# Expert rows gathered in turned form, features stationary

## The chip, the cores and the metric

The kernel runs on one core of a Trainium2 chip. TensorE (PE) multiplies: each product is a load of weights, the stationary operand, into the array (LDWEIGHTS, shown as the engine PEld), and a pass of the moving operand through it (MATMUL). VectorE (DVE), ScalarE (ACT) and GpSimd (POOL) do the rest, SyncE (SP) issues the DMAs. Products accumulate in the eight banks of PSUM, of 512 floats per partition each; everything else lies in SBUF, 128 partitions wide. The metric is the device time of one launch in microseconds.

## The reference

One layer of a hybrid decoder: a token mixer (RG-LRU and linear attention), then a mixture of experts with 32 experts, of which each token takes 4, and a final norm. 280 tokens (16 meta, 256 of the prompt, 8 samples) with 1024 features go through it. The change lies in the expert part:

```python
def _moe(u, w_router, b_router, w_gu, b_gu, w_down, b_down):
    logits = u @ w_router + b_router
    top_val, top_idx = lax.top_k(logits, TOP_K)      # 4 of 32
    gates = jax.nn.softmax(top_val, axis=-1)
    ...
    def expert_block(args):
        tok, e = args
        xb = u_pad[tok]                               # the rows of expert e
        gu = xb @ w_gu[e] + b_gu[e]                   # 1024 -> 2048
        gate = jnp.minimum(gu[:, :D_FF], SWIGLU_LIMIT)
        lin = jnp.clip(gu[:, D_FF:], -SWIGLU_LIMIT, SWIGLU_LIMIT)
        act = (lin + 1.0) * gate * jax.nn.sigmoid(SWIGLU_ALPHA * gate)
        return act @ w_down[e] + b_down[e]            # 1024 -> 1024
    ...
    y = jnp.zeros((n_tok + 1, d)).at[row_tok].add(y_rows * row_w[:, None])
```

## The kernel before

The mixer, the residual and the router come first, until about 165 us. They leave the normalised tokens in `u2` (three chunks of 128, 128 and 24 rows by 1024 features), and for every token and expert its place among the expert's tokens in `pos`. Then come 32 rounds, one for an expert, with room for 64 tokens (S = 64). Everything is in fp32.

Work on one expert is spread over three rounds. In round i, TensorE does, in the order of `body(i)`:
- the gate-up product of expert i, `gu` (L1384): feature blocks k = 0 to 7 of the gathered rows `xT` as weights (128 features by 64 tokens), the expert's `w_gu` moving, 512 columns at a time. Two products of 64 weight columns stand side by side in the array, for the two halves of the columns; they go to PSUM banks 0 and 1. Between its quarters stand
- the scatter of expert i-2 (L1405), after k = 3: products that add its weighted result to the token rows;
- the gather of expert i+1 (L1364), after k = 5. A one-hot matrix `sel` (tokens by 64 places) that DVE makes (L988) is the stationary operand, `u2` the moving one, two halves of 512 features side by side; the three chunks add up in bank 5, and the gathered rows come out as 64 places by 1024 features;
- the down product of expert i-1 (L1398), 16 products like those of the gate-up, into bank 4;
- `turn_rows` (L1371): four transposes of the gathered rows into bank 5;
- the transposes of the gates `Gm` (L1420) and of the gate-up result `guS` (L1427).

ACT empties the banks: it copies bank 5 to `xr` behind the gather (`gathered_rows`, L616), banks 0 and 1 to `guS` (L655), bank 4 to `yS` (L662), and, after `turn_rows`, bank 5 to `xT` (`turned_rows`, L623), from which the next round's gate-up product reads its weights. DVE adds biases and clips (L1001 and on), weighs, and adds the scattered rows to `yacc` (L1027).

SP issues the loads of the weights: four pieces of `w_gu` of 2048 KB and four of `w_down` of 1024 KB for each expert. There is one place for each piece; a piece of the next expert is issued once the products on the last one are done (the semaphores `used0`, `used2`, ... `used11`). The order on every engine is written out by hand; semaphores link the engines.

After round 23 comes a break (`middle`), in which the biases of the down product are added for all experts (L1434, L1444). The last round, `finish`, has no gather. So there are 31 gathers in the rounds, beside the first one, which `first_rows` (L1325) makes between the router's products.

Of the kernel before, what the change touches and what calls it, by code (L numbers as in the profile page):

```python
# [5 lines left out]
def hybrid_layer_kernel(nc, A, O):  # L6
# [8 lines left out]
    ACT = mybir.ActivationFunctionType  # L15
    AX = mybir.AxisListType

    P = 128
# [14 lines left out]
    KD = D // P  # L33
    MA = DA // P
    HP = HB // 2
    TC = 3
# [5 lines left out]
    S = 64  # L42
# [11 lines left out]
    with ctx:  # L54
        sems = {}

        def sem(name):

            if name not in sems:
                sems[name] = ctx.enter_context(nc.semaphore(name))  # L60
            return sems[name]

        def sb(stack, name, shape, dt=fp32):
            return stack.enter_context(nc.sbuf_tensor(name, shape, dt))
# [4 lines left out]
        ident = sb(ctx, "ident", [P, P])  # L69
# [25 lines left out]
        u2 = sb(me, "u2", [P, TC, D])  # L95
        xr = sb(me, "xr", [P, 512])
        sel = sb(me, "sel", [P, TC, S])
        xT = sb(me, "xT", [P, 4, 2, S])
# [16 lines left out]
        ps = ctx.enter_context(nc.psum_tensor("ps", [P, 8, 512], fp32))  # L115
# [47 lines left out]
        at = early.at - 20 - MA * XW - 4 * MA * NB  # L163
        rr = early.ap[:, at:at + MA * NT].rearrange("p (m n) -> p m n", m=MA)
        at = MA * 32
# [62 lines left out]
        rows_of = [P, P, TL]  # L228
# [172 lines left out]
        def lags(i):  # L401

            n = i if isinstance(i, int) else NE
            return n >= 1, n >= 2
# [48 lines left out]
        def _(act):  # L453
# [157 lines left out]
            def gathered_rows(n):  # L611

                act.wait_ge(sem("gathered"), n + 1)
                if not isinstance(n, int) or n >= 1:
                    act.wait_ge(sem("x_turned"), n)
                act.activation(xr[:, :], ps[:, 5, :], ACT.Copy).then_inc(sem("xr_ready"), 1)  # L616

            def turned_rows(n):

                act.wait_ge(sem("x_turned"), n + 1)  # L620
                if not isinstance(n, int) or n >= 1:
                    act.wait_ge(sem("used6"), n)
                act.activation(xT[:, :, :, :].rearrange("p q h s -> p (q h s)"), ps[:, 5, :], ACT.Copy).then_inc(sem("xT_ready"), 1)  # L623

            gathered_rows(0)
            turned_rows(0)
            act.wait_ge(sem("bgu_turned"), 2)
            act.activation(bguT[:, :, :], ps[:, 3, :].rearrange("p (f e) -> p f e", f=NF), ACT.Copy).then_inc(sem("bgu_ready"), 1)
            def middle():
# [4 lines left out]
            def body(i):  # L634
                do_j, do_m = lags(i)

                if do_j:
                    act.wait_ge(sem("clipped"), i)
                    act.wait_ge(sem("product"), i)
                    act.activation(hS[:, 0, :], hS[:, 0, :], ACT.Sigmoid, scale=ALPHA).then_inc(sem("sig_ready"), 1)  # L640
                gathered_rows(i + 1)
                gu_rows(i)
                if do_j:
                    down_rows(i)
                turned_rows(i + 1)
                if do_j:
                    act.wait_ge(sem("gt_turned"), i)
                    act.activation(GT[:, :], ps[:, 6, 0:TC * P], ACT.Copy).then_inc(sem("GT_ready"), 1)

            def gu_rows(i):  # L650

                act.wait_ge(sem("used6"), i + 1)
                if not isinstance(i, int) or i >= 1:
                    act.wait_ge(sem("gu_turned"), i)
                act.activation(guS[:, :].rearrange("p (a n) -> p a n", a=2), ps[:, 0:2, :], ACT.Copy).then_inc(sem("guS_ready"), 1)  # L655

            def down_rows(i):

                act.wait_ge(sem("used11"), i)
                if not isinstance(i, int) or i >= 2:  # L660
                    act.wait_ge(sem("scattered"), TC * (i - 1))
                act.activation(yS[:, :], ps[:, 4, :], ACT.Copy).then_inc(sem("yS_ready"), 1)  # L662
# [413 lines left out]
        def _(pe):  # L1076
# [41 lines left out]
            for j in range(2):  # L1118
                for g in range(4):
                    last = pe.matmul(ps[32 * g:32 * g + 32, 7, 0:NT], wlr[:, 2 * g + j, :], uT[:, 2 * g + j, :], start=(j == 0), stop=(j == 1))  # L1120
# [4 lines left out]
            for m in range(MA):  # L1125
                last = pe.transpose(ps[:, 6, 128 + 32 * m:128 + 32 * m + 32], cst[0:32, m * P:(m + 1) * P], ident[0:32, 0:32])
# [24 lines left out]
            for p in range(2):  # L1151
                pe.wait_ge(sem("rg_sig"), p + 1)
                for k in range(KD):
                    last = pe.matmul(ps[:, 4 + p, :], uT[:, k, NM + 2 * p * CH:NM + 2 * (p + 1) * CH], wv_in[:, k, :], start=(k == 0), stop=(k == KD - 1))  # L1154
# [3 lines left out]
            for j in range(2):  # L1158
                for g in range(4):
                    last = pe.matmul(ps[32 * g:32 * g + 32, 6, :], uX[:, 2 * g + j, :], wv_in[:, 2 * g + j, :], start=(j == 0), stop=(j == 1))  # L1160
# [4 lines left out]
            for q in range(2):  # L1165
                for a in range(HP):
                    last = pe.transpose(ps[:, 0, (2 * q + a) * P:(2 * q + a + 1) * P], kD[:, a, NM + 2 * q * CH:NM + 2 * (q + 1) * CH], ident[:, :])
            last.then_inc(sem("turned"), 1)
            for a in range(HP):
                last = pe.transpose(ps[0:NM, 1, a * P:(a + 1) * P], kD[:, a, 0:NM], ident[:, :])  # L1170
# [7 lines left out]
            for h in range(HB):  # L1178
                a, r = h // 2, slice(64 * (h % 2), 64 * (h % 2) + 64)
                pe.matmul(ps[0:NM, 2 + h % 2, 128 + a * NM:128 + (a + 1) * NM], kIl[r, a, :], qI[r, a, 0:NM], start=True, stop=True)  # L1180
            for q in range(2):
                if q == 1:
                    pe.wait_ge(sem("kv_ready"), KV["keys"])
                for i in range(NSB):
                    for a in range(HP):
                        for r in range(2):
                            t0 = (2 * q + r) * CH
                            for half in range(2):
                                rows = slice(64 * half, 64 * half + 64)
                                last = pe.matmul(ps[64 * r:64 * r + 64, 2 - 2 * q + half, a * CH + SB * i:a * CH + SB * (i + 1)], kI[rows, a, i, t0:t0 + CH],  # L1190
                                                 qI[rows, a, NM + t0 + SB * i:NM + t0 + SB * (i + 1)], start=True, stop=True)
# [6 lines left out]
            for c in range(NCH + 1):  # L1198
                r, q = (c - 1) % 2, (c - 1) // 2
                rows = slice(0, NM) if c == 0 else slice(64 * r, 64 * r + 64)  # L1200
                for h in range(HB):
# [4 lines left out]
                    last = pe.matmul(ps[o:o + 64, 0 if c == 0 else 6 + r, col:col + DV], keys, values, start=True, stop=True)  # L1206
# [4 lines left out]
            for q in range(2):  # L1211
                for a in range(HP):
# [3 lines left out]
                    for half in range(2):  # L1216
                        for r in range(2):
                            h, rows = 2 * a + half, slice(64 * r, 64 * r + 64)
                            col = (q * HB + h) * CH
                            last = pe.matmul(ps[:, 2 + r, col:col + CH], VT[rows, q, h * DV:(h + 1) * DV], PT[rows, q, h, :], start=False, stop=(half == 1))  # L1220
            for h in range(HB):
                last = pe.matmul(ps[:, 1, h * NM:(h + 1) * NM], VTm[0:NM, h * DV:(h + 1) * DV], PTm[0:NM, h, :], start=True, stop=True)
# [5 lines left out]
            for m in range(MA):  # L1228
                last = pe.transpose(ps[0:NO, 7, m * P:(m + 1) * P], OT[:, m, :], ident[:, :])
            last.then_inc(sem("turned"), 1)  # L1230
            pe.wait_ge(sem("sample_state"), 1)
            for j in range(4):
                for g in range(4):
                    a, b = j // 2, 4 * (j % 2) + g
                    last = pe.matmul(ps[32 * g:32 * g + 32, 0, j * DV:(j + 1) * DV], qSp[:, a, b, :], Sn[:, b, a, :], start=True, stop=True)
# [4 lines left out]
            for j in range(4):  # L1240
                last = pe.transpose(ps[:, 6, j * P:(j + 1) * P], soT[:, j * P:(j + 1) * P], ident[:, :])
# [6 lines left out]
            for h in range(HB):  # L1248
                last = pe.matmul(ps[:, h, 0:NT], ones[:, :], tt[:, h, :], start=True, stop=True)
# [48 lines left out]
            for k in range(KD):  # L1298
                last = pe.transpose(ps[:, 5, k * TL:(k + 1) * TL], yacc[0:TL, 2, k * P:(k + 1) * P], ident[0:TL, 0:TL])
# [55 lines left out]
            for c in range(2):  # L1355
                last = pe.matmul(ps[:, 2, 0:NE], ones[:, :], mk[:, c, :], start=False, stop=(c == 1))
            last.then_inc(sem("count_done"), 1)

            def gather(n):

                pe.wait_ge(sem("sel_ready"), n + 1)
                for c in range(TC):
                    for w in range(2):
                        last = pe.matmul(ps[S * w:S * w + S, 5, :], sel[:, c, :], u2[:, c, w * 512:(w + 1) * 512], start=(c == 0), stop=(c == TC - 1))  # L1364
                last.then_inc(sem("gathered"), 1)

            def turn_rows(n):

                pe.wait_ge(sem("xr_ready"), n + 1)
                for q in range(4):  # L1370
                    last = pe.transpose(ps[:, 5, q * P:(q + 1) * P], xr[:, 2 * P * (q // 2) + q % 2:2 * P * (q // 2 + 1):2], ident[:, :])  # L1371
                last.then_inc(sem("x_turned"), 1)

            turn_rows(0)

            def gu(i, k0, k1):

# [69 lines left out]
            def body(i):  # L1447
                do_j, do_m = lags(i)

                pe.wait_ge(sem("xT_ready"), i + 1)  # L1450
                if do_j:
                    pe.wait_ge(sem("guS_ready"), i)
                gu(i, 0, 2)
                gu(i, 2, 4)
                if do_m:
                    scatter(i)
                gu(i, 4, 6)
                if do_m:
                    pe.wait_ge(sem("added"), TC * (i - 2) + 2)
                gather(i + 1)  # L1460
                gu(i, 6, 8)
                if do_j:
                    pe.wait_ge(sem("act_ready"), i)
                    if do_m:
                        pe.wait_ge(sem("added"), TC * (i - 1))
                    for p in DN:
                        dn(i, p, actT, raw[:, p, :], 4)
                turn_rows(i + 1)
                if do_j:
                    turn_weights(i, 6)  # L1470
                if not do_j:
                    pe.wait_ge(sem("flag_ready"), 1)
                turn_gu(i)
# [55 lines left out]
```

## Time and profile before

| | us |
|---|---|
| median of 3 runs | 1112.66 (1112.14 to 1113.95) |
| the profiled execution | 1113.86 |
| its span, first to last instruction | 1112.1 |
| PE busy | 1075.6 |
| PE weight loads (beside the products) | 443.4 |
| DVE busy | 349.0 |
| ACT busy | 191.0 |
| mean granted TensorE clock | 0.986 |

The rows further down come from one profiled execution. Busy times are sums over the span; which engine sets the time in a stretch is read from the chain of work that ended last, which is followed back from the last instruction. A row like `231.01 3.43 PE ps L1384 x16` in it says: from 231.01 us on, for 3.43 us, sixteen instructions of line 1384 on PE. One fp32 product is two instructions, each a weight load and a matmul, and both stand as such in the counts; a transpose is one. In shapes like `128*64 128x512` the first pair is rows by columns of the weights, the second the moving operand. [...]

### The profile page before, as it was taken

Reading aid. Unit: us, or ns where it says so; the run is one execution under the profiler, and the core shown is the slowest. Engines: PE = TensorE matmul, PEld = TensorE weight load, DVE = VectorE, ACT = ScalarE, POOL = GpSimd, SP = SyncE. Lnnn points to the kernel's source line nnn. Section 1 sums busy time; section 2 is a strip of 40 time slices with the busy share of each in tenths; the row PEclk is TensorE's granted clock in tenths of the full one; section 3 lists DMA queues with packets and bytes.
Section 4 is the critical chain, followed back from the end, with each engine's and each line's share of the span. In section 5 each row is a group of like instructions: output and inputs, shape, how many; then the busy total and the mean of one; then the engine's idle time right before and its main releaser. Section 6 shows DMA issues by size and latency. Waiting matters only on the chain.

```text
span 1112.1 us, 13670 instructions
## 1 busy us (share of the span) xinstructions
PE 1075.6 (97%) x5237; PEld 443.4 (40%) x5237; DVE 349.0 (31%) x652; ACT 191.0 (17%) x310; POOL 15.0 (1%) x39
## 2 busy tenths in 40 slices
PE   6999999999999999999999999999999899999996
PEld 5758553333333333333333333333333233333332
DVE  5855331122222222222222222222221322222224
ACT  3453211111111111111011111111111011111112
POOL 3100000000000000000000000000000000000000
PEclk9999988999999999999999999999998899999999
DMA  9661736999999999999999999999999999999994
GB/s 311 242 186 47 265 151 284 424 426 426 426 428 427 427 425 426 427 425 427 425 427 427 425 423 426 427 427 426 427 428 425 425 425 426 426 427 426 426 423 176
DMA packets 54062, 425.30 MB, mean 382 GB/s; under 512 B 7391, under 2 KB 14166, under 8 KB 21274
## 3 DMA queue, kind: packets, MB, share of 16 engines
q1 hardware_dynamic: 53368, 424.67, 92.0%
q0 software_dynamic: 512, 0.26, 0.1%
q8 instruction: 14, 0.23, 0.1%
q10 hardware_dynamic: 162, 0.09, 0.0%
q14 instruction: 6, 0.05, 0.0%
HBM read 422.69 MB, written 2.35 MB: 382 GB/s over the span
## 4 chain that ended last, share of the span: by engine, by line
PE 67%; DMA 31%; DVE 1%; issue 1%; ACT 0%; SPq 0%; DVEq 0%
DMA raw<-in_w_gu 30%; PE ps L1384 29%; PE ps L1398 12%; PE ps L1108 6%; PE ps L1405 5%; PE ps L1364 4%; PE ps L1266 3%; PE ps L1427 2%; PE ps L1154 1%; PE ps L1371 1%; DMA wv<-in_w_in 1%; PE ps L1444 1%; PE ps L1420 1%; PE ps L1325 0%; PE ps L1290 0%
## 5 line engine op out<-in xcount | busy, mean ns | idle before, releaser
L1384 PE MATMUL ps<-raw,xT 128*64 128x512 f32 x2048 | 466.5, 601 | 17.9 <-DMA raw<-in_w_gu 14.2
L1384 PEld LDWEIGHTS ps<-raw,xT 128*64 128x64 f32 x2048 | 141.5, 138 | 311.4 <-issue 280.4
L1398 PE MATMUL ps<-raw,actT 128*64 128x512 f32 x992 | 218.3, 592 | 0.0
L1001 DVE TENSOR_TENSOR hS<-ps,bguT 128x512 f32<-128x512 f32 x64 | 41.2, 686 | 360.0 <-PE ps L1427 359.3
L1027 DVE TENSOR_TENSOR yacc<-ps,yacc 128x1024 f32<-128x1024 f32 x93 | 108.1, 1218 | 137.2 <-PE ps L1405 137.2
L1398 PEld LDWEIGHTS ps<-raw,actT 128*64 128x64 f32 x992 | 71.2, 137 | 141.2 <-issue 141.0
L616 ACT ACTIVATE xr<-ps 128x512 f32<-128x512 f32 x32 | 19.1, 597 | 403.0 <-PE ps L1364 401.4
L1405 PE MATMUL ps<-yS,GT 64*128 64x512 f32 x372 | 88.2, 606 | 0.0
L1364 PE MATMUL ps<-u,sel 128*64 128x512 f32 x372 | 85.1, 592 | 0.0
L988 DVE TENSOR_TENSOR sel<-slot_no,pos 128x192 f32<-128x192 f32 x32 | 11.5, 358 | 154.8 <-PE ps L1364 154.8
L1405 PEld LDWEIGHTS ps<-yS,GT 64*128 64x128 f32 x372 | 33.3, 186 | 54.4 <-issue 54.4
L655 ACT ACTIVATE guS<-ps 128x1024 f32<-128x1024 f32 x32 | 32.8, 1024 | 98.9 <-PE ps L1384 98.9
L662 ACT ACTIVATE yS<-ps 128x512 f32<-128x512 f32 x31 | 18.6, 600 | 178.0 <-PE ps L1398 178.0
L1364 PEld LDWEIGHTS ps<-u,sel 128*64 128x64 f32 x372 | 26.7, 137 | 53.1 <-issue 53.1
L640 ACT ACTIVATE hS<-hS 128x512 f32<-128x512 f32 x30 | 18.9, 629 | 108.7 <-DVE hS L1008 108.7
L1427 PE MATMUL ps<-ident,guS 128*128 128x128 f32 x256 | 36.1, 284 | 0.5 <-ACT guS L655 0.5
L1108 PE MATMUL ps<-uT,wv 128*128 128x280 f32 x128 | 32.8, 418 | 2.8 <-DMA wv<-in_w_in 2.8
L1427 PEld LDWEIGHTS ps<-ident,guS 128*128 128x128 f32 x256 | 33.2, 208 | 1.5 <-ACT guS L655 0.8
L1108 PE MATMUL ps<-uT,raw 128*128 128x280 f32 x128 | 31.6, 402 | 0.0
L1108 PEld LDWEIGHTS ps<-uT,wv 128*128 128x128 f32 x128 | 25.2, 199 | 9.7 <-DMA wv<-in_w_in 3.1
L1266 PE MATMUL ps<-wv,proj 128*128 128x512 f32 x64 | 28.8, 598 | 0.0
L1371 PEld LDWEIGHTS ps<-ident,xr 128*128 128x128 f32 x128 | 18.2, 211 | 25.1 <-issue 25.1
(307 smaller groups left out, 550.3 us busy)
## 6 DMA issues: line engine op xcount, KB each, us to landing
raw<-in_w_gu SPq DMA_DIRECT2D x128, 2048.0 KB, 21.0
raw<-in_w_down SPq DMA_DIRECT2D x128, 1024.0 KB, 22.5
wv<-in_w_in SPq DMA_DIRECT2D x3, 2048.0 KB, 13.7
raw<-in_w_in SPq DMA_DIRECT2D x2, 2048.0 KB, 21.6
wv<-in_w_out SPq DMA_DIRECT2D x1, 4096.0 KB, 14.0
wv<-in_state_gla SPq DMA_DIRECT2D x8, 128.0 KB, 2.4
wv<-v_rows SPq DMA_DIRECT2D x4, 256.0 KB, 5.3
out_gla_s<-wv SPq DMA_DIRECT2D x8, 128.0 KB
```

The source lines that it names most:

```text
L616: act.activation(xr[:, :], ps[:, 5, :], ACT.Copy).then_inc(sem("xr_ready"), 1)
L655: act.activation(guS[:, :].rearrange("p (a n) -> p a n", a=2), ps[:, 0:2, :], ACT.Copy).then_inc(sem("guS_ready"), 1)
L1001: dve.tensor_tensor(hS[:, n, :].rearrange("p (k s) -> p k s", k=8), turned[:, n], bguT[:, 8 * n:8 * n + 8, bass.ds(e_of(i - 1), 1)].broadc ...
L1027: dve.tensor_tensor(dst, ps[:, PAIR[c]:PAIR[c] + 2, :], dst, ALU.add).then_inc(sem("added"), 1)
L1108: last = pe.matmul(ps[:, bank_of(t), 0:NT], w(k), uT[:, k, :], start=(k == K_ORDER[0]), stop=(k == K_ORDER[-1]))
L1266: last = pe.matmul(ps[:, 2 * c + n, :], mixed(k)[:, c * P:c * P + P], wout[:, k, n * 512:(n + 1) * 512], start=(k == 0), stop=(k == KD - 1))
L1364: last = pe.matmul(ps[S * w:S * w + S, 5, :], sel[:, c, :], u2[:, c, w * 512:(w + 1) * 512], start=(c == 0), stop=(c == TC - 1))
L1371: last = pe.transpose(ps[:, 5, q * P:(q + 1) * P], xr[:, 2 * P * (q // 2) + q % 2:2 * P * (q // 2 + 1):2], ident[:, :])
L1384: last = pe.matmul(ps[S * w:S * w + S, n, :], xT[:, k % 4, k // 4, :], raw[:, k, col:col + 512], start=(k == 0), stop=(k == KD - 1))
L1398: last = pe.matmul(ps[S * w:S * w + S, bank, :], acts[:, k, :], weights[:, col:col + 512], start=(k == 0), stop=(k == KD - 1))
L1405: last = pe.matmul(ps[:, PAIR[c] + n, :], weights[S * n:S * n + S, c * P:(c + 1) * P], values[S * n:S * n + S, :], start=start, stop=stop)
L1427: last = pe.transpose(ps[:, 2 + f // 4, (f % 4) * P:(f % 4 + 1) * P], guS[:, 2 * P * (f // 2) + f % 2:2 * P * (f // 2 + 1):2], ident[:, :])
```

## The change

The gathers in the rounds are turned around: `u2` is the stationary operand, in blocks of 128 features by the rows of a chunk, and `sel` the moving one, with 64 columns. What comes out in bank 5 is already features by places, so it is copied to `xT` at once; the copy to `xr` and the four transposes go. For each of the eight feature blocks there are three products, one a chunk, and the third is over the 24 rows that it has. The columns of `u2` are taken with a step of two, as the transposes took those of `xr`. The first gather stays as it was, with its copy and transposes. The diff:

```diff
             def gathered_rows(n):
 
                 act.wait_ge(sem("gathered"), n + 1)
-                if not isinstance(n, int) or n >= 1:
-                    act.wait_ge(sem("x_turned"), n)
-                act.activation(xr[:, :], ps[:, 5, :], ACT.Copy).then_inc(sem("xr_ready"), 1)
-
-            def turned_rows(n):
-
-                act.wait_ge(sem("x_turned"), n + 1)
-                if not isinstance(n, int) or n >= 1:
-                    act.wait_ge(sem("used6"), n)
+                act.wait_ge(sem("used6"), n)
                 act.activation(xT[:, :, :, :].rearrange("p q h s -> p (q h s)"), ps[:, 5, :], ACT.Copy).then_inc(sem("xT_ready"), 1)
...
+                gu_rows(i)
                 gathered_rows(i + 1)
-                gu_rows(i)
                 if do_j:
                     down_rows(i)
-                turned_rows(i + 1)
...
             def gather(n):
 
                 pe.wait_ge(sem("sel_ready"), n + 1)
-                for c in range(TC):
-                    for w in range(2):
-                        last = pe.matmul(ps[S * w:S * w + S, 5, :], sel[:, c, :], u2[:, c, w * 512:(w + 1) * 512], start=(c == 0), stop=(c == TC - 1))
+                for k in range(KD):
+                    columns = slice(2 * P * (k // 2) + k % 2, 2 * P * (k // 2 + 1), 2)
+                    at = (2 * (k % 4) + k // 4) * S
+                    for c in range(TC):
+                        r = rows_of[c]
+                        last = pe.matmul(ps[:, 5, at:at + S], u2[0:r, c, columns], sel[0:r, c, :], start=(c == 0), stop=(c == TC - 1))
                 last.then_inc(sem("gathered"), 1)
...
                     for p in DN:
                         dn(i, p, actT, raw[:, p, :], 4)
-                turn_rows(i + 1)
                 if do_j:
                     turn_weights(i, 6)
```

On TensorE, this is the second part of a round in the loop before, from the second half of the gate-up product on: the gather is L1364, with `sel` as weights, the transposes of the gathered rows L1371.

```order
L1384 MATMUL ps<-raw,xT 64x512 x8
L1459 ISA
L1361 REGISTER_ALU
L1364 MATMUL ps<-u,sel 64x512 x6
L1384 MATMUL ps<-raw,xT 64x512 x8
L1465 REGISTER_ALU
L1393 ISA
L1398 MATMUL ps<-raw,actT 64x512 x16
L1371 MATMUL ps<-ident,xr 128x128 x4
L1418 REGISTER_ALU
L1420 MATMUL ps<-ident,Gm 128x128 x3
L1427 MATMUL ps<-ident,guS 128x128 x8
```

The same stretch now (the gather is L1360, the gate-up product L1376, the down product L1390):

```order
L1376 MATMUL ps<-raw,xT 64x512 x8
L1451 ISA
L1354 REGISTER_ALU
L1360 MATMUL ps<-sel,u 128x64 x24
L1376 MATMUL ps<-raw,xT 64x512 x8
L1457 REGISTER_ALU
L1385 ISA
L1390 MATMUL ps<-raw,actT 64x512 x16
L1410 REGISTER_ALU
L1412 MATMUL ps<-ident,Gm 128x128 x3
L1419 MATMUL ps<-ident,guS 128x128 x8
```

Six products of 512 columns have become 24 of 64, in the same place, and the four transposes behind the down product are gone.

On ACT, a round in the loop before, from the sigmoid (L640) to the copy of the turned gates (L648):

```order
L640 ACTIVATE hS<-hS 128x512
L613 REGISTER_ALU
L615 REGISTER_ALU
L616 ACTIVATE xr<-ps 128x512
L655 ACTIVATE guS<-ps 128x1024
L661 ISA
L662 ACTIVATE yS<-ps 128x512
L623 ACTIVATE xT<-ps 128x512
L648 ACTIVATE GT<-ps 128x384
```

And now (sigmoid L634, `guS` L648, `xT` L615):

```order
L634 ACTIVATE hS<-hS 128x512
L645 REGISTER_ALU
L648 ACTIVATE guS<-ps 128x1024
L613 REGISTER_ALU
L615 ACTIVATE xT<-ps 128x512
L654 ISA
L655 ACTIVATE yS<-ps 128x512
L641 ACTIVATE GT<-ps 128x384
```

The copy to `xr` is gone, and the copy to `xT` has moved from behind the one to `yS`, which waits for the down product, to behind the one to `guS`, which waits for the gate-up product.

## Rows read from the trace of the kernel before

**Rows 1.** The page's fourth part: shares of the chain that ended last, by engine.

```profile
PE 67%; DMA 31%; DVE 1%; issue 1%; ACT 0%; SPq 0%; DVEq 0%
```

**Rows 2.** The chain by time, one round: start us, us, what.

```profile
214.10 0.96 PE ps L1427 x8
...
222.07 2.78 PE ps L1405 x12
224.85 3.58 PE ps L1384 x16
228.44 2.58 PE ps L1364 x12
231.01 3.43 PE ps L1384 x16
234.44 6.87 PE ps L1398 x32
...
242.32 0.96 PE ps L1427 x8
```

**Rows 3.** The chain by time: first products, rounds after 448 us, last transposes before the break.

```profile
168.03 13.30 PE ps L1384 x48
...
448.05 25.65 DMA raw<-in_w_gu
...
477.57 25.65 DMA raw<-in_w_gu
...
851.95 0.96 PE ps L1427 x8
```

**Rows 4.** Groups by line and form: count, busy us, mean ns of one, idle before.

```profile
L1364 PE MATMUL ps<-u,sel 128*64 128x512 f32 x372 | 85.1, 592 | 0.0
...
L1427 PEld LDWEIGHTS ps<-ident,guS 128*128 128x128 f32 x256 | 33.2, 208 | 1.5 <-ACT guS L655 0.8 <-issue 0.7
...
L1420 PEld LDWEIGHTS ps<-ident,Gm 128*128 128x128 f32 x96 | 11.7, 145 | 1.6 <-issue 1.6
...
L1290 PEld LDWEIGHTS ps<-late 128*128 128x128 f32 x32 | 3.8, 192 | 0.5 <-issue 0.5
...
L1356 PEld LDWEIGHTS ps<-late,ones 128*128 128x128 f32 x4 | 0.9, 322 | 0.1
```

**Rows 5.** Weight loads in order of time, router's product: start us, us, engine, line, operands, count.

```profile
146.97 1.75 PEld L1290 LDWEIGHTS ps<-late 128*128 128x128 f32 x15 [0.24 <-issue]
```

**Rows 6.** Weight loads in order of time where 24 and 128 rows take turns.

```profile
152.65 0.29 PEld L1319 LDWEIGHTS ps<-late,ones 24*128 24x128 f32 x2
152.98 0.30 PEld L1320 LDWEIGHTS ps<-late,ones 128*128 128x128 f32 x2
153.20 0.30 PEld L1266 LDWEIGHTS ps<-wv,proj 128*128 128x128 f32 x2
```

**Rows 7.** Weight loads in order of time, the transposes at a round's end.

```profile
241.24 0.56 PEld L1371 LDWEIGHTS ps<-ident,xr 128*128 128x128 f32 x4 [0.81 <-issue]
241.71 0.37 PEld L1420 LDWEIGHTS ps<-ident,Gm 128*128 128x128 f32 x3
242.05 1.04 PEld L1427 LDWEIGHTS ps<-ident,guS 128*128 128x128 f32 x8
```

**Rows 8.** ACT in order of time in the same round.

```profile
234.49 1.02 ACT L655 ACTIVATE guS<-ps 128x1024 f32<-128x1024 f32 x1 [2.76 <-PE ps L1384]
241.44 0.60 ACT L662 ACTIVATE yS<-ps 128x512 f32<-128x512 f32 x1 [5.93 <-PE ps L1398]
242.03 0.60 ACT L623 ACTIVATE xT<-ps 128x512 f32<-128x512 f32 x1
```

**Rows 9.** Stretches: us, PE, PEld, DVE, ACT, POOL busy, granted clock, DMA, GB/s.

```profile
83.40:88.60 5.20, 5.20 (x51) 4.36 (x50) 4.70 (x7) 0.40 (x1) 0.00 (x0) 1.00 0.04 7
...
155.00:160.00 5.00, 5.00 (x40) 4.44 (x40) 2.56 (x10) 2.78 (x5) 0.00 (x0) 1.00 0.10 26
...
160.00:166.00 6.00, 5.46 (x15) 2.04 (x16) 2.74 (x15) 0.88 (x2) 0.00 (x0) 0.50 0.00 0
...
170.00:180.00 10.00, 10.00 (x41) 3.06 (x40) 0.00 (x0) 0.00 (x0) 0.00 (x0) 0.82 0.45 161
...
857.00:858.00 1.00, 1.00 (x2) 0.33 (x1) 0.05 (x1) 0.00 (x0) 0.00 (x0) 0.50 1.00 426
```

**Rows 10.** Weight loads in order of time while the clock was 0.50.

```profile
165.37 0.93 PEld L1356 LDWEIGHTS ps<-late,ones 128*128 128x128 f32 x4
```

More of the change, by code:

```diff
@@ L613, in gathered_rows @@
                 act.wait_ge(sem("gathered"), n + 1)
-                if not isinstance(n, int) or n >= 1:
-                    act.wait_ge(sem("x_turned"), n)
-                act.activation(xr[:, :], ps[:, 5, :], ACT.Copy).then_inc(sem("xr_ready"), 1)
-            def turned_rows(n):
-                act.wait_ge(sem("x_turned"), n + 1)
-                if not isinstance(n, int) or n >= 1:
-                    act.wait_ge(sem("used6"), n)
+                act.wait_ge(sem("used6"), n)
                 act.activation(xT[:, :, :, :].rearrange("p q h s -> p (q h s)"), ps[:, 5, :], ACT.Copy).then_inc(sem("xT_ready"), 1)
-            gathered_rows(0)
-            turned_rows(0)
+            act.wait_ge(sem("gathered"), 1)
+            act.activation(xr[:, :], ps[:, 5, :], ACT.Copy).then_inc(sem("xr_ready"), 1)
+            act.wait_ge(sem("x_turned"), 1)
+            act.activation(xT[:, :, :, :].rearrange("p q h s -> p (q h s)"), ps[:, 5, :], ACT.Copy).then_inc(sem("xT_ready"), 1)
             act.wait_ge(sem("bgu_turned"), 2)
@@ L1361, in gather @@
                 pe.wait_ge(sem("sel_ready"), n + 1)
-                for c in range(TC):
-                    for w in range(2):
-                        last = pe.matmul(ps[S * w:S * w + S, 5, :], sel[:, c, :], u2[:, c, w * 512:(w + 1) * 512], start=(c == 0), stop=(c == TC - 1))
-                last.then_inc(sem("gathered"), 1)
[L1367 to L1374, printed above, removed]
+                for k in range(KD):
[4 more added lines that the diff above has]
+                        last = pe.matmul(ps[:, 5, at:at + S], u2[0:r, c, columns], sel[0:r, c, :], start=(c == 0), stop=(c == TC - 1))
+                last.then_inc(sem("gathered"), 1)
+            pe.wait_ge(sem("xr_ready"), 1)
+            for q in range(4):
+                last = pe.transpose(ps[:, 5, q * P:(q + 1) * P], xr[:, 2 * P * (q // 2) + q % 2:2 * P * (q // 2 + 1):2], ident[:, :])
+            last.then_inc(sem("x_turned"), 1)
             def gu(i, k0, k1):
```

## The prediction

> **What bounds the kernel now.** I read the chain of work that ended last first, since it tells which engine each stretch waits for. It is mostly TensorE, with a block of DMA in the middle [rows 1]. In order of time the expert part has two kinds of rounds. Up to 448 us, and again after the break at 852 us, a round is TensorE work without a gap: from one start of the transposes of guS to the next, 214.10 to 242.32 us, it takes 28.22 us [rows 2]. From 448 us on, the chain runs over the transfers of w_gu, and a round takes 477.57 - 448.05 = 29.52 us [rows 3], because an expert's weights don't come faster. So TensorE has nothing to spare in the first kind, and 29.52 - 28.22 = 1.30 us in the second. From 214.10 to 851.95 us [rows 2, 3] lie 22 rounds, which at 28.22 us would be 620.8 us and took 637.85. TensorE's waiting for weights thus costs 17.0 us of the whole run. This is all that a longer round could hide in.
>
> **What the change removes.** In each of 31 rounds (372 recorded gather instructions, 12 a round [rows 4]) the gather of 12 instructions with 512 columns goes, 2.58 us on the chain [rows 2]. The four transposes of xr go with it: their weight loads start at 241.24 and the next ones at 241.71, so 0.47 us [rows 7]. The entry into full-width transposes after the down product stays, it then falls on the transposes of Gm. ACT loses the copy to xr, which cost nothing, since ACT is idle most of the time. Removed on TensorE: 3.05 us a round.
>
> **What it adds.** 24 products for 8 feature blocks and 3 token chunks; an fp32 product is two instructions here (the old gather's 6 products stand as 12), so 48 pairs of a weight load of 128 columns and a product of only 64 columns.
> The price of such a pair: the nearest row is the router's product, 128x128 weights and 32 columns. 15 weight loads lie in 1.75 us, the last of 0.192 us included, so they start (1.75 - 0.19) / 14 = 0.111 us apart [rows 4, 5]. A product of 64 columns would need 2.58 / 6 / 8 = 0.054 us by the old gather (two instructions run side by side there, 512 columns in 0.43 us), so the load decides, not the columns: 48 x 0.111 = 5.35 us.
> [...]
>
> The third token chunk has 24 rows, the others 128, and each block goes 128, 128, 24. What a change of row count costs is seen where the ranks are computed: products of 24 and of 128 rows take turns, and the two loads of one product start 152.98 - 152.65 = 0.33 us after those of the product before, while two products of one row count stand 153.20 - 152.98 = 0.22 us apart [rows 6]. So a change costs 0.11 us, there are 8 + 7 of them, 1.65 us.
> Entry and exit: the old gather had the shape of the gate-up product around it (128 rows, 64 weight columns), the new one hasn't. The scatter, which changes shape too, takes 2.78 us for 12 instructions where the old gather took 2.58, and the gate-up products behind it 3.58 instead of 3.43 [rows 2]: 0.20 + 0.15 = 0.35 us.
> The weights are read with a step of two floats. Transposes with that step start (1.04 - 0.208) / 7 = 0.119 us apart, those without (242.05 - 241.71) / 3 = 0.113 us [rows 4, 7]: 0.006 more, 0.3 us for 48. No row shows a plain product with such weights. Below it is bounded by nothing added, above by the mean lengths of the loads, 208 ns against 145 for the contiguous ones of Gm [rows 4], that is 0.43 x 5.35 = 2.3 us. I take 0.3, by the distances, since distances and not lengths add up.
> New gather: 5.35 + 1.65 + 0.35 + 0.3 = 7.65 us. A round grows by 7.65 - 3.05 = 4.60 us, to 32.8 us.
>
> **Waits that move.** The copy to xT on ACT now stands behind the copy to guS and before the one to yS. guS is copied from 234.49 for 1.02 us, xT would follow for 0.60 us, done at about 236.1, while the gate-up products that need it come after 243 us [rows 2, 8]: it lies under the down product (6.87 us), and yS behind it still waits for that product's end. In the first round there is no down product; there the transposes of guS (0.96 us) cover the 0.6 us. If that cover were gone, 0.6 us a round would show, 19 us in all. The next one-hot on DVE waits for the gather and starts some 5 us later, with nothing behind it before the next transposes of guS. DMA: a round of 32.8 us is longer than the 29.52 us that the weights take, so the queue on SP waits for TensorE and each piece lands with time to spare; the 17.0 us of waiting vanish.
>
> **The sum.** The profiled execution took 1113.9 us (span 1112.1 and 1.8 us around it; the median of the runs is 1112.7, 1.2 less, which is below anything argued here). 31 x 4.60 = 142.6 us are added, 17.0 us of waiting go: 1113.9 + 142.6 - 17.0 = 1239.5, forecast **1240 us**. With entry, exit and step at nothing it is 31 x 0.65 = 20 us less, 1220; with the step at its upper end 62 us more, 1302. That is this case's own range. DMA then stops setting anything in the loop, and TensorE's weight loads are what the round waits for.
>
> **Rival 1: the clock falls in the gather.** The granted clock isn't constant. [...] If it falls 5 us into each gather, the last 2.65 us run at the half clock's distances, (0.93 - 0.32) / 3 = 0.20 us a load where 0.32 is a load's length there [rows 4, 10], 1.8 times 0.111, which costs 2.1 us; then 5.6 us of gate-up and down products at half speed lose 2.8 us. 4.9 us a round, 31 x 4.9 = 152: 1392 us; 1316 if every second gather is hit.
> [...]
>
> **Rival 2: a cheaper gather.** If the change of row count costs nothing, because the 24-row weights can be loaded while other products run, 31 x 1.65 = 51 us go, and the time is about 1190 us. Loads (5.35 - 1.65) / 48 = 0.077 us apart would give the same. Against it stand the steady 0.33 us of the alternating products [rows 6] and the 0.111 us of loads with next to no columns behind them [rows 5]. [...]
>
> **Rival 3: not slower.** If weight loads vanish behind the products, 48 x 0.054 = 2.6 us replace 2.58 and the transposes are a plain gain of 0.47 us. In the rounds that wait for DMA that is no gain, and those before 448 us only reach them sooner; about 8 rounds after the break stay, 3.7 us: 1110 us. It decides from where a new gather costs no more than 3.05 + 17.0 / 31 = 3.6 us, 75 ns a pair. The row of 111 ns with 32 columns, which are shorter still, speaks against it.
>
> **How the numbers follow.** Forecast case 0.46, rival 1 0.42 (in every gather or in part of them), rival 2 0.06, rival 3 0.02, 0.04 for what I don't see. The range goes from the low end of the forecast case, 1220, to 1415, which takes in the forecast and most of rival 1; left out are rivals 2 and 3 and the upper part of rival 1. About 0.2% is what a measurement of this kernel can tell from no change; faster by that 0.02, within it 0.01, slower 0.97.
>
> **What would show it.** In the profile of the changed kernel: 1488 recorded gather products of 128x64; weight loads of the gather 0.11 to 0.12 us apart, 0.33 us at each change of row count; 7.3 to 7.9 us of chain per gather; rounds of about 32.8 us from first to last, with no piece of DMA in the chain between 200 and 1200 us; xT copied right after guS. A granted clock of 0.50 inside or behind the gathers, and a mean clearly under 0.98, would mean rival 1. A round under 31.6 us would mean rival 2, one under 29.5 us rival 3. DMA still in the chain would show the sum wrong at its base.

## The result and the profile after

The changed kernel takes 1382.5 us (median of 5 runs, 1381.3 to 1390.1) against 1112.7 us: 1.2435 times the time, 95% interval 1.2413 to 1.2458. It is slower, as forecast, and inside the range, but by 270 us and not by the 127 us of the forecast case. The time is close to that of rival 1, 1392 us.

The page of the profiled execution (1390.1 us, span 1388.4 us): busy time and share by engine; then, from its fourth part, the shares of the chain that ended last, by engine and by line. The gate-up product is now L1376, the gather L1360, the down product L1390.

```profile
PE 1365.5 (98%) x6229; PEld 692.9 (50%) x6229; DVE 349.1 (25%) x652; ACT 169.6 (12%) x279; POOL 15.0 (1%) x39
...
PE 98%; DMA 1%; DVE 1%; issue 0%; ACT 0%; SPq 0%; DVEq 0%
PE ps L1376 37%; PE ps L1360 24%; PE ps L1390 16%; PE ps L1397 6%; PE ps L1101 5%; PE ps L1419 2%; PE ps L1259 2%; PE ps L1412 1%; PE ps L1147 1%; DMA wv<-in_w_in 1%; PE ps L1436 1%; PE ps L1318 0%; PE ps L1283 0%; DVE raw L1056 0%; PE ps L1140 0%
```

DMA has gone from 31% of the chain [rows 1] to 1%: every round is now TensorE's from end to end. The gather, 4% of the chain before, is 24%.

One round of the chain by time (start us, us, what), for comparison with [rows 2]:

```profile
740.28 10.77 PE ps L1360 x48
751.05 5.12 PE ps L1376 x16
756.18 6.87 PE ps L1390 x32
763.05 0.48 PE ps L1412 x3
763.52 0.95 PE ps L1419 x8
764.48 7.02 PE ps L1376 x32
771.50 2.78 PE ps L1397 x12
774.27 3.58 PE ps L1376 x16
777.86 2.24 PE ps L1360 x13
```

From one gather's start to the next it is 777.86 - 740.28 = 37.58 us, where 32.8 were forecast. Two pieces are longer than the sum had them: the gather, 10.77 us, and the quarter of the gate-up product behind it, 5.12 us, which took 3.43 before [rows 2]. Nothing was done to that product. The stretches of this round (us, then busy PE, PEld, DVE, ACT, POOL, granted clock as a share of full speed, DMA share, GB/s) say why:

```profile
740.00:744.00 4.00, 4.00 (x26) 3.32 (x24) 0.00 (x0) 0.00 (x0) 0.00 (x0) 0.99 0.97 414
744.00:754.00 10.00, 10.00 (x34) 6.93 (x36) 0.36 (x1) 0.00 (x0) 0.00 (x0) 0.50 0.60 257
754.00:778.00 24.00, 24.00 (x115) 8.54 (x111) 7.70 (x12) 3.12 (x5) 0.00 (x0) 1.00 0.87 354
```

About four microseconds into the gather the granted clock goes to 0.50 and stays there for 10 us, over the rest of the gather and most of the product behind it. This happens in all 31 rounds, for 10 us in nearly all of them. The two pages show it in their second part, the granted clock in 40 slices of the span (in tenths; 9 is 90% or more), first before and then after:

```profile
PEclk9999988999999999999999999999998899999999
...
PEclk9999878888888888888888888888887888888889
```

The clock is back at 1.00 from 754 us on, while the rest of the gate-up product, the down product and the rest of the round run. A TensorE that shows as busy all the time can still lose its clock: from 744 to 754 us it was busy for 10.00 of 10.00 us, at a granted clock of 0.50.

The copy to `xT` went where it was expected, right behind the one to `guS`, and shows in no chain (ACT in order of time):

```profile
756.23 1.02 ACT L648 ACTIVATE guS<-ps 128x1024 f32<-128x1024 f32 x1 [25.57 <-PE ps L1376]
757.15 0.59 ACT L615 ACTIVATE xT<-ps 128x512 f32<-128x512 f32 x1
763.18 0.60 ACT L655 ACTIVATE yS<-ps 128x512 f32<-128x512 f32 x1 [5.44 <-PE ps L1390]
```

### The profile page after: what moved, and what is told of

Read it like the earlier page. It is cut to its first block, busy times and chain, and to the rows that moved or that the text cites. A ratio compares the mean times of both kernels' runs of the same rounds, so it can differ in the third digit from the quotient of the medians.

```text
span 1388.4 us, 15621 instructions
## 1 busy us (share of the span) xinstructions
PE 1365.5 (98%) x6229; PEld 692.9 (50%) x6229; DVE 349.1 (25%) x652; ACT 169.6 (12%) x279; POOL 15.0 (1%) x39
## 4 chain that ended last, share of the span: by engine, by line
PE 98%; DMA 1%; DVE 1%; issue 0%; ACT 0%; SPq 0%; DVEq 0%
PE ps L1376 37%; PE ps L1360 24%; PE ps L1390 16%; PE ps L1397 6%; PE ps L1101 5%; PE ps L1419 2%; PE ps L1259 2%; PE ps L1412 1%; PE ps L1147 1%; DMA wv<-in_w_in 1%; PE ps L1436 1%; PE ps L1318 0%; PE ps L1283 0%; DVE raw L1056 0%; PE ps L1140 0%
## 5 line engine op out<-in xcount | busy, mean ns | idle before, releaser
L1376 PE MATMUL ps<-raw,xT 128*64 128x512 f32 x2048 | 520.6, 662 | 3.8 <-issue 3.1
L1360 PE MATMUL ps<-sel,u 128*128 128x64 f32 x1488 | 331.1, 367 | 0.0
L1360 PEld LDWEIGHTS ps<-sel,u 128*128 128x128 f32 x1488 | 282.4, 254 | 68.0 <-issue 25.2
L1376 PEld LDWEIGHTS ps<-raw,xT 128*64 128x64 f32 x2048 | 153.1, 152 | 321.2 <-issue 312.8
L1390 PE MATMUL ps<-raw,actT 128*64 128x512 f32 x992 | 218.2, 592 | 0.0
L1390 PEld LDWEIGHTS ps<-raw,actT 128*64 128x64 f32 x992 | 69.6, 137 | 142.9 <-issue 142.8
L648 ACT ACTIVATE guS<-ps 128x1024 f32<-128x1024 f32 x32 | 32.7, 1023 | 811.1 <-PE ps L1376 811.1
L1101 PE MATMUL ps<-uT,wv 128*128 128x280 f32 x128 | 32.8, 418 | 2.6 <-DMA wv<-in_w_in 2.6
L634 ACT ACTIVATE hS<-hS 128x512 f32<-128x512 f32 x30 | 18.9, 630 | 110.4 <-DVE hS L1001 110.4
L1008 DVE TENSOR_SCALAR Gm<-slot_no,pos,gate 128x128 f32<-128x128 f32 x96 | 27.4, 342 | 1.5 <-PE ps L1412 1.5
L1101 PEld LDWEIGHTS ps<-uT,raw 128*128 128x128 f32 x128 | 23.9, 190 | 5.8 <-issue 0.4
```

The costliest lines, as they stand in the source:

```text
L1008: dve.tensor_scalar(Gm[:, c, :], slot_no[:, :], pos[:, c, bass.ds(i - 1, 1)], gate[:, c, bass.ds(e_of(i - 1), 1)], ALU.is_equal, ALU.mult) ...
L1101: last = pe.matmul(ps[:, bank_of(t), 0:NT], w(k), uT[:, k, :], start=(k == K_ORDER[0]), stop=(k == K_ORDER[-1]))
L1360: last = pe.matmul(ps[:, 5, at:at + S], u2[0:r, c, columns], sel[0:r, c, :], start=(c == 0), stop=(c == TC - 1))
L1376: last = pe.matmul(ps[S * w:S * w + S, n, :], xT[:, k % 4, k // 4, :], raw[:, k, col:col + 512], start=(k == 0), stop=(k == KD - 1))
L1390: last = pe.matmul(ps[S * w:S * w + S, bank, :], acts[:, k, :], weights[:, col:col + 512], start=(k == 0), stop=(k == KD - 1))
```

## The experiments

Theory 1: the gather stands in each round as one long, thin stretch of TensorE, in which the array spends its time on loading weights and on changes of row count and streams little; that brings the clock down. Against it: the clock follows something else (the round as a whole, the loads, the length), or the pairs are simply dearer than the rows of before say.

**The same gather in three parts.** The 48 pairs and their order stay; only other products stand between them. `gather` now takes the feature blocks that it is to do (that part of the edit isn't shown).

```diff
-                gather(i + 1)
+                gather(i + 1, range(0, 3))
                 gu(i, 6, 8)
+                gather(i + 1, range(3, 6))
...
-                    for p in DN:
+                    for p in DN[:2]:
                         dn(i, p, actT, raw[:, p, :], 4)
+                gather(i + 1, range(6, KD))
+                if do_j:
+                    for p in DN[2:]:
+                        dn(i, p, actT, raw[:, p, :], 4)
```

> The changed kernel with its gather cut into three parts: feature blocks 0 to 2 where the gather stood, 3 to 5 behind the last quarter of the gate-up product, 6 and 7 in the middle of the down product; the same 48 pairs. Theory 1 (the clock falls because one long thin stretch of TensorE stands in every round): no fall in the rounds, granted clock 1.00 there, gather at its full-clock price of about 7.9 us as the changed kernel shows it before its falls, and two more entries and exits of 0.35 us: a round of 28.2 - 3.05 + 7.9 + 1.05 = 34.1 us, time 1114 + 31 x 5.9 - 17 = 1280 us. Theory 2 (the clock follows the whole round's share of short products, wherever they stand): falls stay, 1380 to 1410 us. Theory 3 (the clock takes nothing, the pairs are simply dearer): as theory 2 in time, 1390 us and more.

Measured: 1277.1 us, 1.1462 (1.1435 to 1.149) of the kernel before. That is 105 us less than the changed kernel, with the same products. Theory 1 holds, with a remainder. The granted clock, mean 0.971, still fell in some two rounds of five (13 of 31), for 3.4 us each, so the time of the expectation without a fall was met with falls: the parts cost less than it had put down. Stretches of such a round:

```profile
272.00:281.00 9.00, 9.00 (x51) 5.67 (x50) 0.00 (x0) 1.02 (x1) 0.00 (x0) 1.00 0.95 371
281.00:284.40 3.40, 3.40 (x9) 1.00 (x10) 0.00 (x0) 0.00 (x0) 0.00 (x0) 0.50 0.97 318
284.40:306.00 21.60, 21.60 (x107) 8.85 (x105) 8.05 (x13) 2.21 (x4) 0.00 (x0) 1.00 0.96 367
```

**Four parts.** To be rid of this remainder, two feature blocks each, in four places.

```diff
-                gather(i + 1)
+                gather(i + 1, range(0, 2))
                 gu(i, 6, 8)
+                gather(i + 1, range(2, 4))
...
-                    for p in DN:
+                    for p in DN[:2]:
                         dn(i, p, actT, raw[:, p, :], 4)
+                gather(i + 1, range(4, 6))
+                if do_j:
+                    dn(i, DN[2], actT, raw[:, DN[2], :], 4)
+                gather(i + 1, range(6, KD))
+                if do_j:
+                    dn(i, DN[3], actT, raw[:, DN[3], :], 4)
```

> The changed kernel with its gather cut into four parts of two feature blocks: where it stood, behind the gate-up product, in the middle of the down product and before the down product's last quarter; the same 48 pairs and changes of row count. It is to show the price of the change at full clock. By the run in three parts, whose rounds without a fall took 33.5 us, a gather costs 7.9 us and each part 0.15 us behind it: a round of 28.2 - 3.05 + 7.9 + 0.6 = 33.7 us. Theory 1 (short parts between dense products bring no fall at all): granted clock 1.00 in the rounds, 1114 + 31 x 5.5 - 17 = 1267 us, and the changed kernel's 1382 us are some 130 us of clock. If falls of 3.4 us stay as with three parts, 1285 to 1295 us.

Measured: 1263.8 us, 1.1356 (1.1337 to 1.1375). The granted clock was 1.00 from 196 us to the break, and again from 985 us on. It fell once in the loop, for 3.4 us in the first round (0.84 over 190 to 192 us, 0.65 over 192 to 196); that round has no down product, and its last three parts stand one behind the other, 5.92 us from 185.41. A hundred microseconds in the middle of the run, then a round of its chain (the parts of the gather are L1361):

```profile
600.00:700.00 100.00, 100.00 (x499) 46.45 (x497) 24.09 (x39) 9.69 (x15) 0.00 (x0) 1.00 0.95 375
```

```profile
271.72 1.98 PE ps L1361 x12
273.70 3.58 PE ps L1378 x16
277.28 1.98 PE ps L1361 x12
279.26 3.58 PE ps L1392 x16
282.84 1.98 PE ps L1361 x12
284.82 1.87 PE ps L1392 x8
286.68 1.98 PE ps L1361 x12
288.66 1.87 PE ps L1392 x8
...
305.34 1.98 PE ps L1361 x12
```

A round is 305.34 - 271.72 = 33.62 us. The gather takes 4 x 1.98 = 7.92 us, and each part makes the products behind it 0.15 us longer (3.58 for 3.43). In one place it would be three times 0.15 less, 33.17 us; that, and what is worked out from it here, is an estimate, since no run kept the clock with this gather in one place. So at full clock the change costs 33.17 - 28.22 = 4.95 us a round, and the whole run would take 1113.9 + 31 x 4.95 - 17.0 = 1250 us. The rest of the changed kernel's time, some 1382.5 - 1250 = 132 us, is then the clock: 37.58 - 33.17 = 4.4 us in each round.

**No change of row count.** The third chunk is taken over all 128 rows; the rows above 24 are zero.

```diff
                     for c in range(TC):
-                        r = rows_of[c]
-                        last = pe.matmul(ps[:, 5, at:at + S], u2[0:r, c, columns], sel[0:r, c, :], start=(c == 0), stop=(c == TC - 1))
+                        last = pe.matmul(ps[:, 5, at:at + S], u2[:, c, columns], sel[:, c, :], start=(c == 0), stop=(c == TC - 1))
```

> The changed kernel with the third token chunk taken over 128 rows, of which 104 are zero, so that no product changes the row count. Theory 1: 48 loads 0.117 us apart are 5.6 us, 0.35 for entry and exit, the stretch is denser and shorter and the clock stays at 1.00: 1114 + 31 x (5.97 - 3.05) - 17 = 1187 us. Rival (any stretch of this length that is bound by weight loads brings the clock down): the clock still falls in the rounds, about 4 us a round more, 1290 to 1310 us. Rival (the row count costs nothing): no change against the changed kernel, 1380 us.

Measured: 1182.1 us, 1.0617 (1.06 to 1.0635). In the chain the gather is one piece of 5.80 us, the product behind it takes 3.58 again instead of 5.12, and the round is 297.00 - 265.94 = 31.06 us:

```profile
265.94 5.80 PE ps L1359 x48
271.74 3.58 PE ps L1375 x16
...
297.00 5.80 PE ps L1359 x48
```

The weight loads of that gather in order of time, and the stretch with the next one:

```profile
265.87 5.73 PEld L1359 LDWEIGHTS ps<-sel,u 128*128 128x128 f32 x48 [0.81 <-issue]
```

```profile
297.00:303.00 6.00, 6.00 (x51) 5.86 (x52) 0.06 (x1) 0.00 (x0) 0.00 (x0) 1.00 1.00 426
```

The loads start (5.73 - 0.196) / 47 = 0.118 us apart (0.196 is the mean of one), and the clock holds at 1.00 through a gather of nearly 6 us in one place. A block of six pairs thus takes 0.71 us without changes of row count. In the run in four parts it takes 0.99 (1.98 for two blocks), with two changes to a block if the step from the 64-column products into each part is counted as one; so a change costs 0.14 us.

**Full rows, half the columns.** The same 48 loads, but each product streams 32 columns; half of an expert's places are left out. The edit is against the kernel with full rows, as are the last two below.

```diff
-                        last = pe.matmul(ps[:, 5, at:at + S], u2[:, c, columns], sel[:, c, :], start=(c == 0), stop=(c == TC - 1))
+                        last = pe.matmul(ps[:, 5, at:at + S // 2], u2[:, c, columns], sel[:, c, 0:S // 2], start=(c == 0), stop=(c == TC - 1))
```

> As the kernel with full rows, but each product moves 32 columns in place of 64: half of an expert's 64 places aren't gathered, the other halves of the blocks keep what stood in the bank. The 48 weight loads are the same. Theory 1 (what counts for the clock is how much the array streams, not the loads or the length): the time at full clock is the same as with 64 columns, but the clock falls in the rounds again, about 1290 to 1320 us. Rival (loads count as work, or the changes of row count brought the clock down): clock 1.00, 1187 us.

Measured: 1280.4 us, 1.1512 (1.1493 to 1.1531). Less work, and 98 us slower than with all columns; a little under the expected span. The stretches of a round whose gather begins at 236.54:

```profile
232.00:240.00 8.00, 8.00 (x52) 4.72 (x48) 2.78 (x3) 0.00 (x0) 0.00 (x0) 1.00 1.01 430
240.00:247.00 7.00, 7.00 (x28) 4.81 (x29) 0.36 (x1) 0.00 (x0) 0.00 (x0) 0.51 0.90 384
247.00:266.00 19.00, 19.00 (x93) 7.07 (x91) 4.72 (x10) 3.12 (x5) 0.00 (x0) 1.00 0.85 339
```

And the weight loads of that gather before the fall:

```profile
236.47 3.26 PEld L1359 LDWEIGHTS ps<-sel,u 128*128 128x128 f32 x27 [0.81 <-issue]
```

They start (3.26 - 0.196) / 26 = 0.118 us apart, as with 64 columns. The fall is back, without any change of row count, and with the loads and their number as they were. So between these two runs it isn't the loads, nor the stretch's length at full clock, nor the row count: it is how much the array streams in it. A fall needs no change of row count. Whether the 24-row products of the changed kernel thin its gather by their few rows too, or only by the time that the changes take, isn't separated by any run: full rows took both away.

**Fewer changes of row count.** The chunks in the order 0, 1, 2 and 2, 1, 0 by turns.

```diff
-                    for c in range(TC):
+                    turn = (0, 1, 2) if k % 2 == 0 else (2, 1, 0)
+                    for c in turn:
                         r = rows_of[c]
-                        last = pe.matmul(ps[:, 5, at:at + S], u2[0:r, c, columns], sel[0:r, c, :], start=(c == 0), stop=(c == TC - 1))
+                        last = pe.matmul(ps[:, 5, at:at + S], u2[0:r, c, columns], sel[0:r, c, :], start=(c == turn[0]), stop=(c == turn[-1]))
```

> The changed kernel with the chunks taken 0, 1, 2 in even blocks and 2, 1, 0 in odd ones, so that the row count changes 8 times in a gather in place of 15. At full clock a change costs 0.26 - 0.117 = 0.146 us there, so a gather is 1.0 us shorter, 31 us in all if nothing else changes. Theory 1: the stretch is still thin, the clock falls in most rounds, 1335 to 1355 us. Should the clock hold, it is 1114 + 31 x 4.2 - 17 = 1227 us. Rival (row count costs nothing): 1380 us.

Measured: 1341.3 us, 1.2053 (1.2033 to 1.2073), 41 us less than the changed kernel, in the stated span. The clock still fell in every round (mean 0.887), for 7 or 10 us. A hundred microseconds of it:

```profile
200.00:300.00 100.00, 100.00 (x462) 49.59 (x460) 17.38 (x29) 9.20 (x14) 0.00 (x0) 0.86 0.82 335
```

Seven changes fewer at 0.14 us are 0.14 x 7 x 31 = 30 us of the 41. So taking half of the changes away gives back their own price and a little of the clock, and doesn't keep the clock up.

**The step of the weights.** Full rows, and the features of a block taken side by side; the features then don't match the weights.

```diff
-                    columns = slice(2 * P * (k // 2) + k % 2, 2 * P * (k // 2 + 1), 2)
+                    columns = slice(P * k, P * (k + 1))
```

> As the kernel with full rows, but the feature blocks are taken as 128 neighbouring columns in place of every second one, so that the features of an expert's rows stand in another order than its weights have them. Only the step of the weights' read changes. Theory (a step of two floats costs the 0.006 us a load that the transposes show): 48 x 0.006 x 31 = 9 us less than with full rows, 1173 us. Rival (the step costs nothing): 1182 us. Rival (it costs what the lengths of the loads suggested, 2.3 us a gather): 1110 to 1125 us, since the round is then as short as the weights' transfers.

Measured: 1175.0 us, 1.0558 (1.054 to 1.0576), 7 us less than with the step. The loads of a gather:

```profile
263.47 5.43 PEld L1359 LDWEIGHTS ps<-sel,u 128*128 128x128 f32 x48 [0.81 <-issue]
```

They start (5.43 - 0.192) / 47 = 0.111 us apart, just as the router's did [rows 5]; the step costs 0.3 us a gather (5.73 against 5.43), what the transposes had shown.

**Two chunks.** Full rows, and the third chunk with its 24 tokens left out.

```diff
-                    for c in range(TC):
-                        last = pe.matmul(ps[:, 5, at:at + S], u2[:, c, columns], sel[:, c, :], start=(c == 0), stop=(c == TC - 1))
+                    for c in range(2):
+                        last = pe.matmul(ps[:, 5, at:at + S], u2[:, c, columns], sel[:, c, :], start=(c == 0), stop=(c == 1))
```

> As the kernel with full rows, but the third token chunk (24 tokens) is left out of the gather: 32 pairs in place of 48, all of 128 rows. 32 x 0.118 + 0.15 = 3.9 us, a round grows by 3.9 - 3.05 = 0.87 us to 29.1 us, less than the 29.5 us of an expert's weights. Theory (the 17 us of waiting for weights hide the growth in the rounds before the break, only some 9 rounds behind it show it): 1114 + 9 x 0.87 + 2 = 1124 us. Rival (nothing hides it): 1114 + 27 = 1141 us.

Measured: 1131.6 us, 1.0159 (1.0142 to 1.0176), between the two figures. The chain shows rounds of 405.39 - 376.22 = 29.17 us and nothing of DMA in them, and an odd row in the break:

```profile
376.22 3.91 PE ps L1359 x32
...
405.39 3.91 PE ps L1359 x32
...
869.70 7.63 issue
```

The hiding is there: 22 rounds before the break grew by 0.95 us each, 21 us, of which 17 had been waits. But in the break TensorE began its next product 7.63 us after the last sum of the biases, with nothing in the profile that it waited for; in the kernel before it was 1.79 us, and it is 1.8 or 1.9 in the other traces here. Without these 5.8 us the run would have taken 1126 us, near the 1124 expected. What holds it there wasn't tried and stays open. Only this one trace shows it; the other three runs lie within 2.4 us of it, with the same mean clock of 0.98. In the gap the trace has packets on the DMA queues that it names "instruction" (q14 between 872 and 874 us, q8 between 874 and 876), while the kernel before has none from 840 us to its start at 865. But the run with full rows has one too, between 912 and 914 us, and waited 1.87 us; so whether TensorE waited for code here isn't shown.

## Why the prediction came out as it did

**What bounds the kernel, and the hidden slack: right.** The 17.0 us of waiting for weights vanished, no DMA stands in the loop's chain, and the rounds are alike. The form of the sum holds in the runs whose clock stayed up (with full rows 1.00 over 175 to 900 us, with four parts but for that one fall) and whose rounds are longer than the weights take: 1113.9 + 31 x (round - 28.22) - 17.0 gives 1185 us for full rows (31.06; measured 1182.1), and 1264 for four parts (33.62; 1263.8).

**The price of a pair: right.** 0.111 us and 0.006 for the step were read from the rows; 0.111 without the step and 0.118 with it were measured. That the load and not the columns decides, up to 64 of them, is shown by the half columns, whose loads at full clock are as far apart: 0.118 us, with 32 columns and with 64.

**The change of row count: too small.** 0.14 us in place of 0.11, 2.1 us a gather in place of 1.65. The rows read had 32 columns behind the loads and the gather has 64; whether that is the difference wasn't tried.

**Entry and exit: a little too large.** 0.30 us for 0.35. The gather with full rows is a piece of 5.80 us, of which 48 loads 0.118 apart are 5.65, so the entry costs 0.15; the product behind it takes 3.58 for 3.43, another 0.15. On the other side the four transposes gave back 0.53 us and not 0.47: from the end of the down product to the transposes of guS it was 242.32 - 241.31 = 1.01 us [rows 2], and is 0.48 now.

Together the forecast case had 4.60 us a round and 1240 us, and the runs give 4.95 and 1250: that part of the working stands, with the change of row count as its largest miss.

**The clock: the step that failed.** The forecast case let the granted clock stay at 1.00 in the gather and gave that 0.46; rival 1, with the fall, had 0.42. The fall came in every round. Rival 1's price for it was close: 4.9 us a round and 152 us, where the runs give 4.4 us and some 132. That it was so close is in part luck. The fall came some 4 us into the gather and not 5, so the gather lost more, 10.77 - 7.92 = 2.85 us for 2.1, and the product behind it less, 5.12 - 3.58 = 1.54 us for 2.8; the two misses nearly cancel. The rival's 5.6 us at half speed were an estimate from the one fall ahead of the rounds: the clock stood at 0.50 from 160 until 173.6 us (0.82 over 170 to 180), 5.6 us after the gate-up products had begun at 168.03 [rows 3, 9]. So the fall was named and roughly sized, and the choice between two near chances went wrong, which made the forecast 127 us of a change of 270. The only row that spoke for a steady clock was the stretch at 83 us, at 1.00 over 5.20 us [rows 9]. That stretch held products of 128 columns beside those of 64, while the gather has none of 128, and a third of its pairs have 24 rows, with a change of row count ahead of them and behind. The nearer row was the one from 155 to 160 us: also weight loads one behind the other (4.44 of 5.00 us), with 32 columns behind most of them, and from 160 us on the clock was 0.50 [rows 9]. The half columns fit that kinship: with the loads as they were (0.118 us apart) and less streamed, the fall was back (0.51 over 240 to 247 us).

**The waits moved: right.** `xT` is ready 5 us before the down product ends; no wait on ACT, DVE or SP entered the chain of the rounds.

**Rivals 2 and 3: wrong**, as expected. Changes of row count are paid for, and weight loads aren't hidden behind 64 columns.

No experiment points to a form of this gather that beats the kernel before. The best whole one, with full rows, is 6% slower: its 48 loads alone take 5.6 us, more than the 3.05 us that gather and transposes took.

## What to carry to other kernels

Before a matrix is turned into the stationary operand, count its weight loads: in fp32, 128 columns cost 0.11 to 0.12 us a load here with 32 or 64 moving columns behind it, and there are two loads a product (the gather's 24 products stand as 48); streaming 64 columns takes 0.054 us by the old gather, so the array streams less than half the time. Don't let a short chunk change the row count between products: padding it with zero rows took the gather from 7.9 to 5.8 us at full clock, and 200 us off the run, of which some 70 are the changes and 130 the clock. And read the granted clock beside a stretch that is busy but streams little: it was 0.50 for 10 us here. If the stretch must stay, try it in short parts between dense products: in four parts of 1.98 us the granted clock was 1.00 over 196 to 960 us.

## What was not expected of the hardware

That TensorE, busy by every row from one end of the round to the other, drops to a granted clock of 0.50 once in each of 31 rounds was held a little less likely than that it doesn't. That halving the work of each product (32 columns for 64) makes the run 98 us longer follows from the same clock. And the clock charges the neighbour too: the gate-up product behind the gather went from 3.43 to 5.12 us without a change to it, and is back at 3.58 where the clock holds.
